# Shifting the streamed tiles of a two-block network by 64 bytes in the scratch memory

## The reference

```
for i in range(2):
    hn = rms_norm(h, ln_mix[i])
    h = h + (gdn_mixer(hn, ...) if i == 0 else sb_mixer(hn, k_sh, v_sh, ...))
    h = h + swiglu(rms_norm(h, ln_ffn[i]), ffn_w_in[i], ffn_w_out[i])
    h = h + (p[i] @ ple_w_proj[i]) * sigmoid(rms_norm(h, ln_ple[i]) @ ple_w_gate[i])
    if i == 0: k_sh, v_sh = shared_kv(h, kv_norm, w_kv, k_norm)
x = h + 0.5 * swiglu(rmsnorm(h), ffn1...)
u_hy, u_rw, g_hy, g_rw = split(rmsnorm(x) @ w_in)
x = x + (sigmoid(g_hy) * hyena(u_hy) + sigmoid(g_rw) * rwkv7(u_rw)) @ w_out
x = rmsnorm(x + 0.5 * swiglu(rmsnorm(x), ffn2...))
```

## Time and profile before

| | |
|---|---|
| median of 3 runs | 3026.94 us |
| span of the profiled execution | 3024.8 us |
| TensorE busy | 2934.6 us, 97% |
| VectorE busy | 1482.9 us, 49% |
| ScalarE busy | 1092.3 us, 36% |
| GpSimd busy | 238.3 us, 8% |
| DMA, mean over the span | 82 GB/s |

### The profile page before, as it was taken

One profiled execution on the slowest core, in us unless ns is written; L12 is line 12 of the kernel. 1 busy time (PEld: TensorE's weight loads), 2 busy tenths in 40 slices (PEclk: granted clock), 3 DMA queues, 4 the chain that ended last, 5 costly groups with the idle time before them and its releaser, 6 DMA issues.

```text
span 3024.8 us, 46853 instructions
## 1 busy us (share of the span) xinstructions
PE 2934.6 (97%) x21214; PEld 2421.7 (80%) x21214; DVE 1482.9 (49%) x1463; ACT 1092.3 (36%) x1186; POOL 238.3 (8%) x135
## 2 busy tenths in 40 slices
PE   8999899999999999999999999999998998999998
PEld 5778778888888788888878888788877887888886
DVE  6765544443355444443454443545667654644432
ACT  5554532222354832222342222442244432332222
POOL 1002110000100010000110000320002220000001
PEclk9999999999999999999999999999999999999999
DMA  3210022223222012222222223221230002222221
GB/s 143 82 61 2 16 84 93 91 96 118 98 87 98 28 70 98 98 98 105 100 96 98 93 98 114 94 77 67 93 114 5 4 5 115 98 94 94 95 108 70
DMA packets 44901, 249.29 MB, mean 82 GB/s; under 512 B 8443, under 2 KB 12283, under 8 KB 17184
## 3 DMA queue, kind: packets, MB, share of 16 engines
q1 hardware_dynamic: 43552, 242.11, 22.7%
q10 hardware_dynamic: 1152, 4.19, 0.3%
HBM read 237.90 MB, written 8.39 MB: 81 GB/s over the span
## 4 chain that ended last, share of the span: by engine, by line
PE 86%; DVE 6%; ACT 4%; issue 2%; POOL 1%; DMA 0%; DVEq 0%; SPq 0%; ACTq 0%; POOLq 0%
PE ps L588 69%; PE ps L2766 7%; PE ps L1409 2%; PE ps L2350 1%; ACT whi L266 1%; PE ps L2334 1%; DVE wlo L272 1%; PE ps L3811 1%; PE ps L2070 1%; PE ps L3792 1%; PE ps L3823 0%; DVE gdn_conv L1043 0%; PE ps L2953 0%; PE ps L2044 0%; PE ps L413 0%
## 5 line engine op out<-in xcount | busy, mean ns | idle before, releaser
L272 DVE TENSOR_TENSOR wlo<-wraw,whi 128x2048 fp32r<-128x2048 f32 x210 | 486.9, 2319 | 939.9 <-ACT whi L266 939.8
L266 ACT ACTIVATE whi<-wraw 128x2048 fp32r<-128x2048 f32 x210 | 402.1, 1915 | 926.7 <-PE ps L588 926.6
L588 PE MATMUL ps<-ffn_xh,whi 128*128 128x512 f32 x1408 | 553.1, 393 | 3.4 <-DVE ffn_xl L389 2.1
L588 PE MATMUL ps<-ffn_xh,wlo 128*128 128x512 f32 x1408 | 552.2, 392 | 0.0
L588 PE MATMUL ps<-ffn_xl,whi 128*128 128x512 f32 x1408 | 548.7, 390 | 0.0
L588 PEld LDWEIGHTS ps<-ffn_xh,whi 128*128 128x128 f32 x1408 | 264.7, 188 | 59.9 <-issue 2.7
L588 PEld LDWEIGHTS ps<-ffn_xl,whi 128*128 128x128 f32 x1408 | 264.6, 188 | 59.6 <-issue 1.0
L588 PEld LDWEIGHTS ps<-ffn_xh,wlo 128*128 128x128 f32 x1408 | 264.7, 188 | 57.8
L588 PE MATMUL ps<-ffn_uh,wlo 128*128 128x512 f32 x704 | 275.8, 392 | 0.0
L588 PE MATMUL ps<-ffn_uh,whi 128*128 128x512 f32 x704 | 275.7, 392 | 0.0
L588 PE MATMUL ps<-ffn_ul,whi 128*128 128x512 f32 x704 | 274.0, 389 | 0.0
(11 more groups left out here) (509 smaller groups left out, 4701.4 us busy)
## 6 DMA issues: line engine op xcount, KB each, us to landing
wraw<-in_weights SPq DMA_DIRECT2D x211, 1024.0 KB, 4.8
gates_kept<-gates_tmp ACTq DMA_DIRECT2D x8, 512.0 KB, 4.2
mix_gate<-gates_kept SPq DMA_DIRECT2D x8, 512.0 KB, 10.7
h<-in_x SPq DMA_DIRECT2D x4, 512.0 KB, 8.5
mix_y<-hz_kept SPq DMA_DIRECT2D x2, 1024.0 KB, 5.9
out<-out SPq DMA_DIRECT2D x4, 512.0 KB, 3.2
wraw<-in_weights SPq DMA_DIRECT2D x2, 512.0 KB, 6.9
ple_raw<-in_p SPq DMA_DIRECT2D x4, 256.0 KB, 5.2
```

What stands on the lines that cost most here:

```text
L266: c.nc.scalar.activation(c.whi[:, j % 2, :], c.wraw[:, j % 2, :], ACT.Copy).then_inc(c.hi_ready, 1)
L272: c.nc.vector.tensor_tensor(c.wlo[:, j % 2, :], c.wraw[:, j % 2, :], c.whi[:, j % 2, :].bitcast(F32), ALU.subtract).then_inc(c.lo_ready, 1)
L588: last = nc.tensor.matmul(pair[:, m, :], a, b, start=opens and n == 0 and wa + xa == 0, stop=closes and n == len(ks) - 1 and wa == 1)
```

## The change

Only numbers in the address book change. The places of the streamed tiles move down or up by 64 bytes: U_AT from 20,544 to 20,480 and S_AT from 110,656 to 110,720, and with U_AT `gdn_x`, `gdn_o`, `kv_x`, `q_x`, `sb_o`, the attention's keys, queries and values and its core's tiles. The square buffers and `gdn_mid` of the first mixer move up by 64. Where the shifted tiles now begin, `gdn_hot`, `rstdT` and `sb_qg` lay before, at 20,480; `gdn_hot` goes to 9,376, the other two to 143,552 and 143,584, behind S_AT's tiles, whose tail also pushes `hy_tpos` and `hy_rsq` up by 64. Not moved are `gdn_qkv` (69,696), `gdn_gate` (53,312), the Hyena tiles `hy_kpm`, `hy_k`, `hy_trig`, `hy_Z`, the recurrence's tiles, and all of feed-forward 3.

No instruction, size, semaphore or order differs: on each of the five engines the rows of both programs stand in the same order, 11,140 on TensorE's queue, 1221 on VectorE's, 1009 on ScalarE's.

The remainders of the streamed tiles by 256, as addresses in SBUF:

| tiles | before | after |
|---|---|---|
| `gdn_x`, `gdn_o`, `ffn_u` (0 to 2), `kv_x`, `q_x`, `sb_o`, `sb_k`, `sb_v`, `sb_q` | 192 | 128 |
| `ffn_x` (0 to 2), `ple_x`, `hy_x` | 192 | 0 |
| `gdn_sqh`, `gdn_sql` | 192 | 0 |
| `ffn3_x`, `ffn3_u`, `mix_m`, `mix_y`, `ple_p`, `sb_sqh`, `sb_sql`, `whi`, `wlo` | 128 | 128 |
| `gdn_hot` | 128 | 32 |
| `ones` | 96 | 96 |

```diff
...
-        self.hot = c.at("gdn_hot", [P, 2 * HEADS - 1], 20480, F32R)
+        self.hot = c.at("gdn_hot", [P, 2 * HEADS - 1], 9376, F32R)
-        self.mid = [c.at(f"gdn_mid{x}", [HEADS, T], 61504 + 2048 * x, F32R) for x in range(3)]
+        self.mid = [c.at(f"gdn_mid{x}", [HEADS, T], 61568 + 2048 * x, F32R) for x in range(3)]
...
-        self.tpos = c.at("hy_tpos", [P, NH + 1], 143424)
+        self.tpos = c.at("hy_tpos", [P, NH + 1], 143488)
...
-        self.rsq = c.at("hy_rsq", [P, 2, NH], 143456)
+        self.rsq = c.at("hy_rsq", [P, 2, NH], 143520)
...
-    x = two(c, "gdn_x", KD, 20544)
+    x = two(c, "gdn_x", KD, 20480)
...
-    scales = Scales(c, qkv_part, qkv, decays, G8, beta8, small, 53312)
+    scales = Scales(c, qkv_part, qkv, decays, G8, beta8, small, 53376)
-    core = DeltaCore(c, qkv, gate, scales, two(c, "gdn_o", KD, 20544))
+    core = DeltaCore(c, qkv, gate, scales, two(c, "gdn_o", KD, 20480))
-U_AT, S_AT = 20544, 110656
+U_AT, S_AT = 20480, 110720
...
-              c.at("ple_pl", [P, 2, T], 14336, F32R), c.at("ple_kept", [P, KD, T], 86080),
-              c.at("ple_sig", [P, 2, T], 102464))
-    rows, qg = c.at("rstdT", [P, T // P], 20480), c.at("sb_qg", [P, 1], 20512)
+              c.at("ple_pl", [P, 2, T], 14336, F32R), c.at("ple_kept", [P, KD, T], 86016),
+              c.at("ple_sig", [P, 2, T], 102400))
+    rows, qg = c.at("rstdT", [P, T // P], 143552), c.at("sb_qg", [P, 1], 143584)
...
-    ple.feed = norm_kv = Norm(c, "kv_n", bufs, "kv_norm", two(c, "kv_x", KD, 20544), ple.ready, rows=rows, halves=True)
-    second = SecondGain(c, "q_x", "ln_mix.1", two(c, "q_x", KD, 53312), norm_kv)
-    k, v, q = c.at("sb_k", [P, HEADS, T], 110656), c.at("sb_v", [P, T // P, DM], 127040), c.at("sb_q", [P, HEADS, T], 86080)
+    ple.feed = norm_kv = Norm(c, "kv_n", bufs, "kv_norm", two(c, "kv_x", KD, 20480), ple.ready, rows=rows, halves=True)
+    second = SecondGain(c, "q_x", "ln_mix.1", two(c, "q_x", KD, 53248), norm_kv)
+    k, v, q = c.at("sb_k", [P, HEADS, T], 110592), c.at("sb_v", [P, T // P, DM], 126976), c.at("sb_q", [P, HEADS, T], 86016)
...
-    o = two(c, "sb_o", KD, 20544)
-    core = StickCore(c, k, q, v, o, v_part, norms[2], 53312, 102464, 18432)
+    o = two(c, "sb_o", KD, 20480)
+    core = StickCore(c, k, q, v, o, v_part, norms[2], 53248, 102400, 18432)
```

## The result

The changed kernel takes 3035.7 us (median of 6 runs, 3032.7 to 3040.3) against 3027.1 us (3026.4 to 3030.1): a ratio of 1.0030 with a 95% interval of 1.0020 to 1.0039. It is slower by 0.3%, where 0.5% faster was forecast. The profiled execution has a span of 3033.2 us and took 3035.1 us, 8.4 us more span than before.

The account below looks back on a forecast made before the run. The prediction took TensorE's dense products (L588) as the bound: 15.2 us from streams moved to even multiples of 64 plus 0.6 from the slow spacing, 3026.9 - 15.8 = 3011.1 us, range 3006 to 3016, with faster at 0.87.

Parts of the forecast that it names:

- What bounds the kernel: Whole kernel: TensorE busy 97%, dense products (L588) 69% of the span, so the time of a streamed matmul there decides.
- The natural comparison: Feed-forwards 0 and 3, same code: 228.91 ns per matmul at remainder 192, 226.71 at 128; 2.19 ns blamed on the address.
- How many matmuls gain: Dense products: 7728 matmuls move from odd to even multiples of 64, 2.19 ns each, 17.0 us; 15.2 us on the path.
- The slow spacing: Query, value and Hyena tiles at 233.5 instead of 229.2 ns, following sums with `ones` at 96; about 1.5 us, -0.6 taken.
- The values' product: Streams even weights against odd stationary tiles; counted only in the slow spacing, two stretches of 0.40 and 0.25 us.
- rival (c): S_AT tiles: remainder 0 in step with stationary 128 gives 233.5 ns, 21.2 us lost, 6.8 gained, 3041 us; chance 0.04.
- Small parts: Attention core's short streams (up to 0.5 us), moved `gdn_hot` (0.1 to 1.7 us) and small tiles: taken as nothing.
- The rule of the Trainium skill: All streamed rows: SBUF lines of 16 bytes, both addresses multiples of 16, so the time stays at 3026.9 us.
- The size: Whole kernel: 15.2 us from the streams plus 0.6 from the slow spacing, 15.8 us off.

Follow-up runs that it names:

- the first experiment: Changed kernel with the S_AT tiles 128 bytes further, at remainder 128 instead of 0, and four small tiles behind them moved to the arena's end: 3017.5 us, ratio 0.9967.

## Why the prediction was wrong

- *What bounds the kernel* held: the total moved with L588's spacing, and apart from stretches at the half clock (1.6 us in the attention core) with nothing else of size. No wait, engine or transfer took part.
- *The natural comparison* was measured rightly: 228.9 against 226.7 ns between feed-forwards 0 and 3. Its reading failed. The prediction took the cause to be the parity of the streamed address and so let every tile that reached an even multiple of 64 gain. Both even places of the trace had remainder 128 by 256, and so had the weights; the trace could not tell "even" from "same as the weights". The two experiments that move the weights separate the two: with every streamed tile in its place, weights moved by 128 or by 64 bytes swap the good and the bad stages.
- *How many matmuls gain* is the failed term: 3120 of the 7728 did, most of them at the forecast 2.2 ns. The 4608 on S_AT went to distance +128 and lost 3.5 to 4.4 ns each: 12.7 us lost in their stages, against 5.3 us gained in those of `ffn_u`, keys, queries and `sb_o`.
- *The slow spacing* of 233 ns in queries and keys did vanish, as was half assumed. Its tiles now take 10.89 us for 48, 226.9 ns, like all others, though the sums ahead of them still run with `ones` at remainder 96; so a misaligned `ones` is not enough to make it:

```profile
907.18 10.89 PE ps L588 x48
```

- *The values' product* was priced within 1.5 us either way as a matter of the slow spacing; it lost 1.8 us since its stationary tile moved. The stationary tile's address stands in the prediction as an open question here and as a half sentence in rival (c), but in no term of the sum.
- *Small parts* held at zero: `gdn_x` behind the moved `gdn_hot` runs at 227.2 ns, and the attention core's float32 streams keep their spacing. The latter had to: their streamed and stationary tiles moved together.
- *The rivals.* Rival (c) came nearest. Its title, "remainder 0 is a bad place", is wrong (with the weights there too it has 226.7 ns), but its reason, a streamed row in step with the stationary one at 128, is about the pair. It had 0.04. That its price of 233.5 ns is near the measured 232.4 is luck in part, since it was borrowed from the slow spacing; its total of 3041 us took 21.2 us for the S_AT tiles where 12.7 were lost. What was held against it was one row of float32 matmuls, of which the prediction itself said that it might hide the effect, and the suspicion against `ones`. That the forecast rested on places at remainder 128 alone, while 60% of the matmuls went to remainder 0, deserved far more doubt, and so a range to 3041.
- *The rule of the Trainium skill* ("SBUF — State Buffer", Specifications), lines of 16 bytes, does not describe this either: all places here are multiples of 16, and the spacing goes from 226.7 to 234.3.
- *The size* of the forecast, tested by the first experiment, where all long streams do gain: 9.6 us (3027.2 to 3017.5) in place of 15.8. The feed-forwards gave 10.9 us of span where 4752 x 2.19 ns = 10.4 were forecast. The first mixer and the Hyena stage together gave 1 us, less than the 2.6 that the sum held for them (1196 of its 6908 matmuls); parts of both go over other engines. The values took back 1.8. The profiled execution of that run, the fastest of its five, is 12.4 us shorter than the one before, so about 3 of the 6 us between 15.8 and 9.6 are scatter of the runs.

What makes the distance matter is not shown. The trace of the kernel before has each stationary tile loaded while the matmul before it streams, so both are read at one time:

```profile
600.08 0.39 PE L588 MATMUL ps<-ffn_xh,whi 128*128 128x512 f32 x1
600.08 0.19 PEld L588 LDWEIGHTS ps<-ffn_xl,whi 128*128 128x128 f32 x1
```

But the run with `wlo` alone moved does not point to that load in a simple way, and no kernel here had streams without loads beside them.

## What to carry to other kernels

When a tight stream of float32r matmuls runs some per cent over its best spacing, compare the addresses of the streamed and of the stationary tile: put both at the same remainder by 256 for 512 columns, and measure again for shorter streams, since 256 columns had another best distance. Never judge an address by one alone; before a shift, list the remainders of both sides for every stage and look whether the trace holds a stage at each of the new pairs. Where it does not, one profile of a kernel with another distance in each stage maps them all.

## What the runs showed of the hardware that was not expected

- The distance between streamed and stationary address moves the spacing of 512-column float32r matmuls between 226.7 and 234.3 ns, with a sign; a further 256 bytes change nothing (`mix_mh` and the x tiles of the first experiment lie at 384 by 512, the weights at 128, and both have 226.7).
- Full float32 matmuls don't show it as far as they were tried: pairs of 512 columns (L413, `norm_acc` with `ones`) take the same 1.02 us at distance +32 and at +160, in the run with the weights at 0. In the attention core the distance never changed, so its 428 ns (L3823) say nothing.

```profile
444.43 1.02 PE L413 MATMUL ps<-norm_acc,ones 128*128 128x512 f32 x2
```

- A misplaced pair costs in a repeating pattern: over three matmuls at +64 (226, 229, 232 ns); at +128 over seven, with one of 241 ns, where the mean is 232.4, and over two (229, 238 ns) where it is 233.3. The pattern holds for hundreds of microseconds.
